# Output projections that begin before the last query tile is finished, in a two-block transformer kernel

## The reference

```
for l in 0, 1:
    hn = rmsnorm(h); proj = hn @ w_in[l]
    do = diff_attention(...)   # 4 heads, two softmaxes each, 128 wide; gated
    fo = forgetting_attention(...)   # 8 heads, 64 wide; gated
    h = h + concat(do, fo) @ w_out[l]
x = rmsnorm(h)[16:]
x = x + 0.5 * swiglu(rms_norm(x))            # ffn1, inner width 2816
h = rms_norm(x)
x = x + concat(nsa(h), stick_breaking(h)) @ w_out
x = x + memory_cross_attention(rms_norm(x), rms_norm(mem)) @ wo   # 4 heads of 64, 256 memory rows
x = x + 0.5 * swiglu(rms_norm(x))            # ffn2
```

## Time and profile before

| | |
|---|---|
| median of 3 runs | 1990.39 us (1989.87 to 1991.45) |
| the profiled execution | 1991.26 us, span 1989.5 us |
| PE busy | 96% of the span |
| DVE, ACT, POOL busy | 39%, 36%, 36% |
| mean granted clock of PE | 0.989 of full |
| HBM | 72 GB/s over the span |

### The profile page before, as it was taken

One profiled execution on the slowest core, in us unless ns is written; L12 is line 12 of the kernel. 1 busy time (PEld: TensorE's weight loads), 2 busy tenths in 40 slices (PEclk: granted clock), 3 DMA queues, 4 the chain that ended last, 5 costly groups with the idle time before them and its releaser, 6 DMA issues.

```text
span 1989.5 us, 26539 instructions
## 1 busy us (share of the span) xinstructions
PE 1914.2 (96%) x10878; PEld 1631.8 (82%) x10878; DVE 779.5 (39%) x1308; ACT 707.3 (36%) x1328; POOL 712.6 (36%) x343
## 2 busy tenths in 40 slices
PE   7999989999998999999999999899999989999999
PEld 6999878989987887888888877789767768888887
DVE  5433373464326436441112255546666441111001
ACT  3112355321225544232222223446565542222211
POOL 4333201353331114555554423320003325555443
PEclk9999899999999999999999999999999989999999
DMA  4222200122221002323332333210003212222223
GB/s 142 85 82 79 65 1 1 56 83 86 85 85 33 1 22 91 95 92 96 92 95 91 98 102 117 66 42 2 1 0 117 75 54 95 96 95 92 94 88 109
DMA packets 40585, 144.22 MB, mean 72 GB/s; under 512 B 4624, under 2 KB 4880, under 8 KB 40336
## 3 DMA queue, kind: packets, MB, share of 16 engines
q1 hardware_dynamic: 40464, 142.51, 22.2%
HBM read 140.40 MB, written 2.10 MB: 72 GB/s over the span
## 4 chain that ended last, share of the span: by engine, by line
PE 86%; DVE 7%; ACT 3%; DMA 2%; issue 1%; POOL 1%; SPq 0%; DVEq 0%; ACTq 0%
PE ps L354 22%; PE ps L355 22%; PE ps L356 22%; PE ps L849 5%; PE ps L830 5%; PE ps L839 3%; DMA raw<-wstream 2%; PE ps L1994 1%; PE ps L1977 1%; ACT wh L342 1%; PE ps L481 1%; PE ps L966 1%; DVE xl L410 1%; PE ps L1966 1%; POOL wl L350 1%
## 5 line engine op out<-in xcount | busy, mean ns | idle before, releaser
L350 POOL TENSOR_TENSOR wl<-raw,wh 128x1024 fp32r<-128x1024 f32 (+2 forms) x254 | 604.0, 2378 | 855.7 <-ACT wh L342 855.7
L354 PE MATMUL ps<-xh,wh 128*128 128x512 f32 (+1 forms) x1728 | 622.4, 360 | 28.1 <-POOL wl L350 12.9
L355 PE MATMUL ps<-xl,wh 128*128 128x512 f32 (+1 forms) x1728 | 615.6, 356 | 0.0
L342 ACT ACTIVATE wh<-raw 128x1024 fp32r<-128x1024 f32 (+2 forms) x254 | 266.0, 1047 | 978.7 <-PE ps L356 906.5
L356 PE MATMUL ps<-xh,wl 128*128 128x512 f32 (+1 forms) x1728 | 613.6, 355 | 0.0
L354 PEld LDWEIGHTS ps<-xh,wh 128*128 128x128 f32 x1728 | 326.9, 189 | 84.4 <-issue 18.8
L355 PEld LDWEIGHTS ps<-xl,wh 128*128 128x128 f32 x1728 | 327.2, 189 | 50.0 <-issue 1.9
L356 PEld LDWEIGHTS ps<-xh,wl 128*128 128x128 f32 x1728 | 327.7, 190 | 48.3
L1093 POOL TENSOR_TENSOR xl<-xb,xh 128x512 fp32r<-128x512 f32 (+1 forms) x22 | 26.1, 1186 | 328.6 <-ACT xh L1002 328.6
L355 PE MATMUL ps<-aL,wh 128*128 128x512 f32 x352 | 139.3, 396 | 0.0
L356 PE MATMUL ps<-aH,wl 128*128 128x512 f32 x352 | 139.1, 395 | 0.0
(11 more groups left out here) (346 smaller groups left out, 2635.2 us busy)
## 6 DMA issues: line engine op xcount, KB each, us to landing
raw<-wstream SPq DMA_DIRECT2D x236, 512.0 KB, 3.5
raw<-wstream SPq DMA_DIRECT2D x16, 384.0 KB, 3.0
raw<-wstream SPq DMA_DIRECT2D x10, 528.0 KB, 3.6
h<-xT SPq DMA_DIRECT2D x4, 528.0 KB, 6.6
out<-h SPq DMA_DIRECT2D x8, 256.0 KB, 3.9
hm<-memT SPq DMA_DIRECT2D x1, 1024.0 KB, 4.8
cst<-const SPq DMA_DIRECT2D x1, 720.5 KB, 9.6
cst<-const SPq DMA_DIRECT2D x1, 320.0 KB, 4.3
```

The source lines that it names most:

```text
L342: e.activation(wh[p % 2][:, 0:n], raw[c % 2][:, 0:n], ACT.Copy).then_inc(*w_hi(p))
L350: e.tensor_tensor(wl[p % 2][:, 0:n], raw[c % 2][:, 0:n], wh[p % 2][:, 0:n].bitcast(F32), ALU.subtract).then_inc(*w_lo(p))
L354: e.matmul(o, w_h, x_h, start=start, stop=False)
L355: e.matmul(o, w_h, x_l, start=False, stop=False)
```

## The change

Five edits:

1. **Layers.** `Plan` names the PE part of the last end (the transposes of `fox` or `mem` tile 3) as `held`, and `attention_pe` leaves it out. `wout_pe` begins column 0 with tokens that need only query tiles 0 to 2, then does the held transposes, then the rest of these tokens, then the last tokens. In layer 0 the 264-token halves are cut as 264, 136 and 128; in layer 1 the 512 tokens as 192, 192 and 128.
2. **mo.** For columns m = 0, 1, 2 the first 384 tokens are multiplied ahead, with the held transposes behind m = 0, then 128 tokens for each of the three, then the other five columns whole.
3. **Order on DVE and ACT.** The addition of column m comes ahead of the low part of column m-1. ACT splits the next weights ahead of the high part of m = 3 and m = 7 instead of behind.
4. **Banks.** The cycle of pairs is set so that ffn2's first tile takes banks 6 and 7.
5. **Norm.** `norm_pe` of ffn2 stands behind the up tile of f = 0 instead of the gate tile, and ACT's Ln and Exp behind the split of the next weights.

```diff
+        def part_of_tile(e, on, key, o, half, lo, hi, x, c0, src):
+            p = PART[key]
+            hh, ll = wh[p % 2], wl[p % 2]
+            th, tl = src
+            on.wait_ge(*w_hi[p])
+            on.wait_ge(*w_lo[p])
+            a, b = c0 + o.shape[2] * half + lo, c0 + o.shape[2] * half + hi
+            for k in range(KT):
+                for s in x(k):
+                    on.wait_ge(*s)
+                r = mm3(e, o[:, half, lo:hi], hh[:, 128 * k:128 * k + 128], ll[:, 128 * k:128 * k + 128],
+                        th[:, k, a:b], tl[:, k, a:b], k == 0, k == KT - 1)
+            return r
...
+        def next_pair(b, of=(0, 2, 4, 6)):
+            turns[of] = of.index(b) - 1
...
+                group = units[-1].group
+                self.held = (group, 1) if group[0] in ("fox", "mem") else None
...
                 for key, k in plan.ends.get(s, []):
-                    end_pe(e, on, plan, key, k)
+                    if (key, k) != plan.held:
+                        end_pe(e, on, plan, key, k)
...
-        def layer_ao(l):
-            return lambda k: [s["ao", "diff" if k < 4 else "fox", l, 3] for s in (x_hi, x_lo)]
+        def layer_ao(l, i=3):
+            return lambda k: [s["ao", "diff", l, 3] if k < 4 else s["ao", "fox", l, i] for s in (x_hi, x_lo)]
 
         def wout_pe(e, on, l):
             n, c0 = shape(l, "out")
-            for _ in residual_pe(e, on, ("wout", l), layer_ao(l), n, c0, pair, X[l]):
-                pass
+            early = [(0, 0, 192), (0, 192, 384)] if l else [(0, 0, 264), (1, 0, 136)]
+            late = (0, 384, 512) if l else (1, 136, 264)
+            key = ("wout", l, 0)
+            claim(on, pair(key), 2 if n > 512 else 1, v_out[key])
+            for i, part in enumerate(early):
+                part_of_tile(e, on, key, out_of(key, n), *part, layer_ao(l, 2), c0, X[l])
+                if i == 0:
+                    end_pe(e, on, plans[l], *plans[l].held)
+            part_of_tile(e, on, key, out_of(key, n), *late, layer_ao(l), c0, X[l]).then_inc(*tile(*key))
+            for c in range(1, KT):
+                key = ("wout", l, c)
+                claim(on, pair(key), 2 if n > 512 else 1, v_out[key])
+                feature_tile(e, on, key, out_of(key, n), n, c0, layer_ao(l), X[l])
...
         def ffn_pe(e, on, st):
+            if st == "ffn2":
+                next_pair(6)
...
-                    if f == 0 and s == 0:
-                        if st == "ffn1":
-                            final_pe(e, on)
-                        else:
-                            norm_pe(e, on, st, T, 1, pair(st), SUMMED(st))
+                    if f == 0 and s == 0 and st == "ffn1":
+                        final_pe(e, on)
+                    if f == 0 and s == 1 and st == "ffn2":
+                        norm_pe(e, on, st, T, 1, pair(st), SUMMED(st))
...
         def ffn_act(e, on, st):
-            if st == "ffn2":
-                norm_act_scale(e, on, st, T, 1, bank[st], 1, rst[:, 0:T])
             for f in range(FT):
                 split_hi(e, on, PART[st + "g", f] + 2)
+                if st == "ffn2" and f == 0:
+                    norm_act_scale(e, on, st, T, 1, bank[st], 1, rst[:, 0:T])
...
             attention_pe(e, on, plans["mem"])
+            for m in range(3):
+                claim(on, pair(("mo", m), SINGLES), 1, v_out["mo", m])
+                mo_cols(m, 0, 384, 2)
+                if m == 0:
+                    end_pe(e, on, plans["mem"], *plans["mem"].held)
+            for m in range(3):
+                mo_cols(m, 384, T, 3).then_inc(*rows("mo", m))
+            for m in range(3, KT):
+                claim(on, pair(("mo", m), SINGLES), 1, v_out["mo", m])
+                mo_cols(m, 0, T, 3).then_inc(*(rows("mo", m) if m % 4 < 3 else tile("mo", m // 4)))
...
             for half in range(2):
                 for m in range(4 * half, 4 * half + 4):
+                    if m % 4 == 3:
+                        split_hi(e, on, PART["mo", half] + 2)
                     gained_hi(e, on, "ffn2", m, h[:, m, M:L], P_("g_ffn2", m, m + 1), xh[:, m, M:L], v_out["mo", m])
-                split_hi(e, on, PART["mo", half] + 2)
...
-            for m in range(KT):
-                on.wait_ge(*mo_done(m))
-                e.tensor_tensor(h[:, m, M:L], h[:, m, M:L], PS[:, 512 * bank["mo", m]:512 * bank["mo", m] + T],
-                                ALU.add).then_inc(*v_out("mo", m))
-                gained_lo(e, on, "ffn2", m, h[:, m, M:L], P_("g_ffn2", m, m + 1), xh[:, m, M:L], xl[:, m, M:L])
+            for m in range(KT + 1):
+                if m < KT:
+                    on.wait_ge(*mo_done(m))
+                    e.tensor_tensor(h[:, m, M:L], h[:, m, M:L], PS[:, 512 * bank["mo", m]:512 * bank["mo", m] + T],
+                                    ALU.add).then_inc(*v_out("mo", m))
+                if m:
+                    gained_lo(e, on, "ffn2", m - 1, h[:, m - 1, M:L], P_("g_ffn2", m - 1, m), xh[:, m - 1, M:L],
+                              xl[:, m - 1, M:L])
```

More of the change, by code:

```diff
@@ L2095, in memory_pe, with mo_cols @@
             attention_pe(e, on, plans["mem"])
[L2096 to L2103, removed]
+            def mo_cols(m, a, b, group):
+                p, w = PART["mo", m // 4], 128 * (m % 4)
+                hh, ll = wh[p % 2], wl[p % 2]
+                on.wait_ge(*w_hi[p])
+                on.wait_ge(*w_lo[p])
+                on.wait_ge(*x_hi["ao", "mem", group])
+                on.wait_ge(*x_lo["ao", "mem", group])
+                o = PS[:, 512 * bank["mo", m] + a:512 * bank["mo", m] + b]
+                for k in range(2):
+                    r = mm3(e, o, hh[:, 512 * k + w:512 * k + w + 128], ll[:, 512 * k + w:512 * k + w + 128],
+                            amh[:, k, a:b], aml[:, k, a:b], k == 0, k == 1)
+                return r
+            for m in range(3):
[8 more added lines that the diff above has]
+                mo_cols(m, 0, T, 3).then_inc(*(rows("mo", m) if m % 4 < 3 else tile("mo", m // 4)))
         def mo_done(m):
```

## The result

The changed kernel takes 1978.32 us (median of 7, 1975.15 to 1985.47) against 1990.39 us (median of 7) of the kernel before on the same chip: ratio 0.9938, interval 0.9922 to 0.9953. A second series of the same kernel gave 1977.68 against 1989.75 (0.9942, 0.992 to 0.9964).

What follows compares the result with a forecast made beforehand. TensorE, busy 1914.2 of 1989.5 us, was taken as the bound. Layers 0.3 + 0.2, plus 9.75 at the ffn2 joint, less 1.6 for clock, gave 8.7 us off: median 1981.7 us, range 1978.5 to 1986.

Steps and rivals of the forecast that it cites:

- Layer 0: Joint of attention and output projection in layer 0: gain 0.3 us (0.1 to 0.6), idle time mostly repaid as weight loads.
- layer 1: Same joint in layer 1: gain 0.2 us (-0.2 to 0.5), already counting that the slow clock is gone.
- rival (c): Narrow matmuls cost only their columns, 0.06 us at 128: 1977.4 us with one slow stretch, 1975.8 without; chance 0.05.
- (d): Narrow matmuls cost more per column, as if each column passed four times: 11 us slower, 2001 us; chance 0.03.
- Case (e): Nothing gained: ffn2's first tile still waits at 1611 for a late bank or weight; 1989 to 1991 us; chance 0.05.
- (b): Both new gaps bring the slow clock, or m=2's low part is held too: 4.4 to 7 us off; chance 0.22.
- I count one: Entry into ffn2: one slow-clock stretch after the two new PE gaps, costing some 8 matmuls x 0.2 = 1.6 us.
- The second is the sum of that joint: From mo into ffn2: the up tile of f=1 starts 9.75 us earlier, less what the clock takes.
- One round costs 0.68 + 0.75 = 1.4 us: VectorE's add and low part per mo column, with ScalarE's high part beside it: 1.4 us instead of 2.1.
- then VectorE 0.69, then a table load of 1.28: Chain after ffn2's norm to f=0's Silu, with VectorE's 0.69 and the 1.28 us load in sequence; Silu done at 1619.7.
- case (a): Rival of no slow clock after the two new gaps at ffn2's entry: 10.3 us off, 1980.1 us; chance 0.25.
- Rival C: The experiments' rival theory for the whole kernel: the clock is what counts; no size or chance given for it overall.

Runs made afterwards that it cites:

- a: Kernel before with only ffn2's first tile moved to banks 6 and 7; 1991.97 us, ratio 1.0006.
- c: Kernel before with both the bank move and the norm behind the up tile, nothing of mo or VectorE's order; 1988.71 us, ratio 0.9995.
- b: Kernel before with only ffn2's norm moved behind the up tile, and Ln and Exp behind the split; 1990.98 us, ratio 0.9998.
- f: Changed kernel without the move of ffn2's first tile to banks 6 and 7; 1979.77 us, ratio 0.9946 to the kernel before.
- h: Changed kernel with ffn2's norm back behind the first gate tile; 1982.30 us, ratio 0.9957 to the kernel before.
- e: Changed kernel with VectorE's old order and ScalarE's splits back behind m=3 and m=7; 1985.24 us, ratio 0.9969 to the kernel before.
- l: The changed kernel measured again, nothing altered; 1977.68 us against 1989.75 of the kernel before.
- i: Changed kernel with the layers' joints filled by k-steps on finished operands, no tile cut by tokens; 1977.21 us, ratio 0.9937 to the kernel before.
- g: Changed kernel with ScalarE's split for the up tile of f=1 ahead of Ln, Exp and Silu of f=0; 1980.61 us, ratio 0.9952 to the kernel before.

## Why the prediction was wrong

**The order of waits was right.** Layer 0: 0.3 forecast, 0.48 measured; layer 1: 0.2 and 0.36. Layer 1's sum took the slow clock of before as given; at full clock, as in a and c, the same edit loses 0.85. The narrow matmuls cost 0.112 to 0.114 us where I took 0.115. The rule of the Trainium skill ("TensorE: Matmul & The Clock Gate", section "Wait — 56ns, not 53.3ns?"), columns / 2.4 GHz plus 2.5 ns, would be 0.056 at 128 columns; the trace has twice that, with 128x128 weights loaded for each matmul. So rival (c) is out, and so is (d). `mo` runs without a gap. The order of waits in ffn2 is the one foretold, k=7 first, then the weights of the up tile of f=1. The edits do not add up: alone, the banks cost 0.8 and the norm gives 0.3 (a, b); taken out of the set they are worth 2.9 and 5.4, and edit 3 is worth 7.5 (f, h, e), in sum 15.8 us, more than the 11.38 of the whole joint. Case (e), nothing gained, is out as well, and so is (b): there was no slow clock at the joint, and the low part of m=2 was not held.

**Two terms were mis-sized.** The first is the clock: "I count one" slow stretch, 1.6 us. The changed kernel has none at this entry, and neither has l; J was 34.66 in both. I had sized the gaps at 1.8 and 2.1 us; they were 1.10 and 1.23. Whether the clock stayed full because they were shorter is not shown.

The second is the sum of that joint, 9.75 forecast, 11.38 measured. The 1.63 us lie in the main at two places. "One round costs 0.68 + 0.75 = 1.4 us": it costs 1.26, since an operation that follows another starts some 0.08 us before the end that the trace gives. With that k=7 came 19.60 us after the last attention group began, not 20.44: 0.84. From the norm's first matmul to the up tile of f=1 I had 1623.35 - 1613.8 = 9.55 us, and it took 8.68: 0.87, mostly because of "then VectorE 0.69, then a table load of 1.28". I put the load behind VectorE's product, while ScalarE loads the table while it waits for that product. The row of before that I used could not show it, for there the load stood behind a split (1623.30 to 1624.34 in the timeline). But the same trace shows it in ffn1, where the load starts 0.48 us before the end of the product that its Silu waits for:

```profile
785.23 0.69 DVE L1366 TENSOR_TENSOR xb<-ps,scratch 128x512 f32<-128x512 f32 x1
785.44 1.28 ACT L1344 ACT_TABLE_LOAD   x1
```

From k=7 to the norm I was 0.08 too low.

Three slips did not change the time. The norm costs PE 1.42 us and not 1.8 (1620.11 to the up tile at 1621.53 in the timeline of before; 1.47 in the changed kernel). Seven k-steps of 0.7 from 1600.5 end at 1605.4 and not at 1605.7. And (363.19 - 358.74) spans 36 matmuls and not 37, 0.124 each, of which the first few are slow; from column 1 on the pitch is 0.121.

Together 8.7 + 1.6 + 1.6 + 0.3 (layers) = 12.2. My case (a), no slow clock, would have been 10.3.

**The range** ended at 1978.5 because it left out the case of no slow clock together with a joint that is better than computed; both errors had the same sign, and I had put bounds only on the unfavourable side of VectorE's timing.

**The clock's part.** Rival C is not the whole story but has a share. Over 35 executions of the kernel before the time falls by 1.3 us for each 0.001 of mean clock (least squares; 0.4 and 0.9 over the 13 and 17 executions on two other chips), and the mean clock is 0.9888 (0.9897 on the other two); over the changed kernel's first seven it is 0.9933. Of the slow stretches in the profile of before, one lies at layer 1's joint, one at `mo` and one at ffn2's first tile, windows of the kernel before:

```profile
1589.00:1594.60 5.60, 3.74 (x10) 2.86 (x11) 0.79 (x2) 0.42 (x1) 0.72 (x1) 0.60 0.00 0
1611.40:1617.40 6.00, 5.94 (x14) 4.71 (x15) 3.81 (x4) 4.35 (x7) 2.39 (x1) 0.50 0.10 29
```

Missing clock is 3.5 x 0.49 + 5.6 x 0.40 + 6.0 x 0.50 = 7.0 us, 0.0035 of the span, which is most of the difference of 0.0045 in the mean clock. They lie inside the joints whose lengths are summed above, so they are not a further gain. No run separates how the 11.38 us of J divide between waits and clock, but the rows of before bound it. The stretch at ffn2's first tile cost nothing: the norm behind that tile started at 1620.11, just after VectorE's last sum, at 1614.14 + 5.92 = 1620.06, and a faster tile would have waited for the same sum. The stretch at `mo` delayed VectorE's first add by some 6 x (0.43 - 0.233) = 1.2 us and its second by the 0.33 it waited for PE. So the clock's share of J is about 1.5 us (an estimate from these rows), and the waits have the rest. With the 11.01 - 9.80 = 1.2 us that it cost in layer 1's joint, its share of the 12.2 is some 2.7 us.

## What to carry to other kernels

Where several waits stand one behind the other at the entry of a stage, list them all with the time at which each would end. An edit that removes the visible one shows the next (6.16 us became 6.20), and the edits have to be valued as a set. A joint can be filled with no extra matmuls by k-steps that need only finished operands, which was worth 2.2 and 2.0 us more in the two layers than cutting the tile by tokens, where each piece loads the weights again. Where the wait is short and the tile wide, as in layer 1, the cut costs more than the wait, unless the clock falls. And when executions differ by 10 us, compare the joint's own length between two marks of the trace: J was 34.66, 34.66 and 34.61 in three traces with the same entry (the changed kernel, l and i), while the medians did not rank the last four kernels. Look at the clock within the joint too: the same joint took 9.80 or 11.01 us.

## What the runs showed of the hardware that was not expected

The same gap is not always followed by the same clock. In the middle stage, outside every edit, PE idles 2.12 us before 1283.58 in the kernel before, and the clock stayed full; in the changed kernel it idles 2.13 us before 1279.64, and the clock is at 0.74 on the mean of the 5 us around it:

```profile
1277.50:1282.50 5.00, 2.87 (x15) 2.86 (x15) 2.76 (x11) 1.93 (x5) 1.08 (x1) 0.74 0.00 0
```

And an attention stage of many small matmuls can run at 1.2 GHz for some 20 us with PE busy throughout, at a price of 8 us. In the profiled execution of the changed kernel the clock was full for the first 2.6 us behind the mark at 1314.77 and 0.50 from 1317.5 to 1337.8; g and i have the same stretch, the other eleven traces do not. What sets it off is not shown. It is most of the difference between the profiled execution at 1985 and the one at 1975.56, whose spans are 9.9 us apart; for executions without a trace only the mean clock is on record.

As forecast, GpSimd's split and VectorE's low part keep each other out: a low part of 0.75 us that starts second takes 2.31 to 2.38. The Trainium skill ("SBUF — State Buffer", on the shared port pair) has it as an exclusive lock, and the trace agrees. What the forecast did not use is that the add, with one operand in PSUM, is not held (0.68 us within GpSimd's 2.41).
